# Feed-forward stages: the two halves of an inner chunk's split one tile apart, and other steps for the first gate row

## The reference, cut to what matters

```python
def swiglu(h, w_gate, w_up, w_down):
    return (jax.nn.silu(h @ w_gate) * (h @ w_up)) @ w_down

mod = (jax.nn.silu(c) @ w_ada[l] + b_ada[l]).reshape(B, N_MOD, D)
m = [mod[:, j] for j in range(N_MOD)]
h = modulate(rmsnorm(x, ffn1_pre_g[l]), m[0], m[1])
y = swiglu(h, ffn1_w_gate[l], ffn1_w_up[l], ffn1_w_down[l])
x = x + 0.5 * m[2][:, None, :] * rmsnorm(y, ffn1_post_g[l])
```

## Time and profile before

| | |
|---|---|
| three runs, us | 2525.47, 2531.29, 2531.94 |
| the profiled execution, us | 2531.54 |
| its span, us | 2529.7 |
| granted TensorE clock, mean | 0.991 |
| busy share of the span | PE 96%, PEld 88%, DVE 66%, ACT 48%, POOL 28% |
| DMA over the span | 457.45 MB, 181 GB/s |

### The profile page before, as it was taken

How to read it: one execution, slowest core, us unless ns; L and a number is a source line. 1 busy time by engine, 2 the same in 40 slices (tenths; PEclk the granted TensorE clock), 3 DMA queues, 4 the chain that set the end, 5 groups by cost and what they waited for, 6 DMA issues and landing times.

```text
span 2529.7 us, 40330 instructions
## 1 busy us (share of the span) xinstructions
PE 2439.4 (96%) x16347; PEld 2233.2 (88%) x16347; DVE 1675.0 (66%) x3111; ACT 1204.4 (48%) x1827; POOL 711.8 (28%) x333
## 2 busy tenths in 40 slices
PE   4999899999999999999999999999999999999999
PEld 3997878988889999999888888889999999888887
DVE  6887775546565787899544445664877899644444
ACT  4444665445654444443444445654444444444443
POOL 3111001112025661000344443115663000244443
PEclk9999999999999999999999999999999999999999
DMA  7988444665345554444565665335554444555554
GB/s 282 327 300 308 162 138 151 216 195 171 109 159 170 169 166 154 139 142 142 191 196 192 194 193 194 127 125 186 165 177 157 137 140 142 181 192 193 193 192 165
DMA packets 126589, 457.45 MB, mean 181 GB/s; under 512 B 13974, under 2 KB 16962, under 8 KB 125635
## 3 DMA queue, kind: packets, MB, share of 16 engines
q1 hardware_dynamic: 121442, 441.52, 52.4%
q10 hardware_dynamic: 4048, 8.91, 1.0%
q0 software_dynamic: 912, 4.42, 0.5%
HBM read 451.62 MB, written 5.93 MB: 181 GB/s over the span
## 4 chain that ended last, share of the span: by engine, by line
PE 79%; DVE 6%; ACT 1%; issue 0%; POOL 0%; ACTq 0%; DVEq 0%; POOLq 0%
PE bank L607 24%; PE bank L609 23%; PE bank L608 23%; PE bank L1170 4%; DVE sb L2612 1%; DVE sb L2608 1%; DVE sb L1846 1%; PE bank L955 1%; PE bank L1146 1%; PE bank L816 0%; ACT sb L1213 0%; DVE sb L2615 0%; PE bank L622 0%; PE bank L1098 0%; PE bank L973 0%
## 5 line engine op out<-in xcount | busy, mean ns | idle before, releaser
L607 PE MATMUL bank<-sb,sb 128*128 128x256 f32 (+1 forms) x4744 | 1523.1, 321 | 49.1 <-DVE sb L1846 37.0
L608 PE MATMUL bank<-sb,sb 128*128 128x256 f32 (+1 forms) x4744 | 1497.3, 316 | 0.0
L609 PE MATMUL bank<-sb,sb 128*128 128x256 f32 (+1 forms) x4744 | 1497.2, 316 | 0.0
L1213 ACT ACTIVATE sb<-sb 128x1024 fp32r<-128x1024 f32 x765 | 806.6, 1058 | 1087.1 <-PE bank L609 1079.7
L2720 POOL TENSOR_TENSOR sb<-sb,sb 128x1024 fp32r<-128x1024 f32 x256 | 644.1, 2519 | 1337.6 <-ACT sb L1213 1333.6
L607 PEld LDWEIGHTS bank<-sb,sb 128*128 128x128 f32 x4744 | 911.5, 192 | 118.8 <-issue 35.4
L1846 DVE TENSOR_TENSOR sb<-sb,sb 128x1024 fp32r<-128x1024 f32 x509 | 626.2, 1231 | 559.6 <-ACT sb L1213 558.3
L608 PEld LDWEIGHTS bank<-sb,sb 128*128 128x128 f32 x4744 | 911.9, 192 | 55.2 <-issue 1.0
L609 PEld LDWEIGHTS bank<-sb,sb 128*128 128x128 f32 x4744 | 911.0, 192 | 55.4
L2684 DVE TENSOR_TENSOR sb<-sb,sb 128x1024 fp32r<-128x1024 f32 x64 | 160.0, 2499 | 149.7 <-ACT sb L1802 149.7
L2647 DVE TENSOR_SCALAR sb<-sb,sb 128x128 f32<-128x128 f32 x512 | 142.2, 341 | 0.0
(11 more groups left out here) (274 smaller groups left out, 1238.7 us busy)
## 6 DMA issues: line engine op xcount, KB each, us to landing
sb<-in_peer_down_dram SPq DMA_DIRECT2D x256, 512.0 KB, 3.3
sb<-in_peer_up_dram SPq DMA_DIRECT2D x256, 512.0 KB, 3.3
sb<-in_w_ada_dram SPq DMA_DIRECT2D x72, 512.0 KB, 6.5
sb<-in_hyb_in_dram SPq DMA_DIRECT2D x56, 512.0 KB, 3.4
sb<-in_ffn_gate_dram SPq DMA_DIRECT2D x44, 512.0 KB, 4.3
sb<-in_ffn_up_dram SPq DMA_DIRECT2D x44, 512.0 KB, 5.2
sb<-in_ffn_down_dram SPq DMA_DIRECT2D x44, 512.0 KB, 4.3
sb<-in_mix_in_dram SPq DMA_DIRECT2D x25, 512.0 KB, 4.1
```

Of the source, the lines that this page charges most:

```text
L607: e.matmul(out, a[0], b[0], start=start, stop=False)
L608: e.matmul(out, a[0], b[1], start=False, stop=False)
L609: return e.matmul(out, a[1], b[0], start=False, stop=stop)
L1213: self.e.activation(rr(M.hi[k % NSPLIT]), M.raw[k % NRAW], AF.Copy).then_inc(*self.S.tick("hi", k))
```

## The change

`hidden` is cut in two on both engines that have it. On ScalarE `hidden` keeps silu and a new `hidden_part` has the copy; on VectorE `hidden` keeps the product and `hidden_part` has the remainder. `hidden_part(j - 1)` is called after the second `linear()` of chunk j, so one tile later than before: behind the split of tile 2j+4 and the step of tile 2j+1. After the last chunk both are called in turn. This holds for ffn1 and ffn2. In ffn1 the steps of rows change from (13, 15, 16, 18) to (13, 19, 21, 24). The waits themselves and all instructions stay as they are.

```diff
-    "ffn1": (... ("ada", tuple(range(62))), ("rows", (13, 15, 16, 18))),
+    "ffn1": (... ("ada", tuple(range(62))), ("rows", (13, 19, 21, 24))),
...
 # ScalarE
         self.e.activation(m.sg[j % 3], self.K.bank["hidden", s, j][:, 0:256], AF.Silu).then_inc(*self.S.tick("silu", s, j))
+
+    def hidden_part(self, j):
+
+        m, s = self.m, self.s
         self.wait_ge("hidden", s, j)
         self.e.activation(rr(m.hid_hi[:, j]), m.hd[j % 3], AF.Copy).then_inc(*self.S.tick("hidden_hi", s, j))
...
 # VectorE
-        self.e.tensor_tensor(h, self.K.bank["hidden", s, j][:, 256:512], m.sg[j % 3], ALU.mult).then_inc(
+        self.e.tensor_tensor(m.hd[j % 3], self.K.bank["hidden", s, j][:, 256:512], m.sg[j % 3], ALU.mult).then_inc(
             *self.S.tick("hidden", s, j))
+
+    def hidden_part(self, j):
+
+        m, s = self.m, self.s
         self.wait_ge("hidden_hi", s, j)
-        self.e.tensor_tensor(rr(m.hid_lo[:, j]), h, m.hid_hi[:, j], ALU.subtract).then_inc(*self.S.tick("hidden_lo", s, j))
+        self.e.tensor_tensor(rr(m.hid_lo[:, j]), m.hd[j % 3], m.hid_hi[:, j], ALU.subtract).then_inc(*self.S.tick("hidden_lo", s, j))
...
 # ScalarE and VectorE, ffn
             if j:
                 self.hidden(j - 1)
             self.linear()
+            if j:
+                self.hidden_part(j - 1)
         self.hidden(NFF - 1)
+        self.hidden_part(NFF - 1)
         self.contract(NFF)
```

More of the change, by code:

```diff
@@ L64 @@
 BESIDE = {
-    "ffn1": (("vectors", (0, 1, 2)), ("bias", (0, 6, 7, 8, 14, 15)), ("ada", tuple(range(62))), ("rows", (13, 15, 16, 18))),
+    "ffn1": (("vectors", (0, 1, 2)), ("bias", (0, 6, 7, 8, 14, 15)), ("ada", tuple(range(62))), ("rows", (13, 19, 21, 24))),
     "mix1": (("recurrence", (4, 9, 10, 12, 13, 14, 15, 16, 17, 18, 19, 20, 21, 22, 23)), ("select", tuple(range(9, 21))),
@@ L2080, in hidden @@
         m, s = self.m, self.s
-        h = m.hd[j % 3]
         self.wait_ge("silu", s, j)
```

## The result

| us | before | after |
|---|---|---|
| median | 2530.89 (5 runs, 2525.47 to 2531.94) | 2515.30 (5 runs, 2513.32 to 2516.80) |
| profiled execution | 2531.54 | 2513.32 (the fastest of the five) |
| first feature transpose after the stage (L622) | 255.58 | 240.01 |

The ratio is 0.9941 with the 95% interval 0.9930 to 0.9951: faster by 15.6 us at the medians. The first stage's end moved by 15.57 us. The second feed-forward stage takes what it took (from the feature transposes ahead of it to those behind it, 377.92 to 576.58, 198.66 us; before 393.56 to 592.31, 198.75), so all that the medians show lies in the first.

What follows compares the result with a forecast made beforehand. VectorE was taken to bound the first feed-forward stage's chunks with two modulation tiles, making TensorE wait. Links 6.2, end of inner chunks 3.0 and gate row 3.6 sum to 12.8 us: 2531.5 − 12.8 = 2518.7, say 2519, range 2512 to 2528.

Steps and rivals of the forecast that it cites:

- The bound: First feed-forward stage: VectorE is the bound in chunks with two modulation tiles, 6.42 us against TensorE's 5.76.
- the second rival: First stage: links do not matter, VectorE stays late for another reason (GpSimd's low parts); gate row alone pays, 2527, chance 0.14.
- The sum: First stage: 6.2 + 3.0 + 3.6 = 12.8 us won, of 15.0 that can be won.
- the gate row: First stage, steps moved: TensorE's wait for this row and its slow matmuls go, 4.1 us less 0.5, so 3.6 won.
- The links: First stage's inner chunks: later copy and remainder end both VectorE stalls; eight of nine short waits go, 6.2 us won.
- nine short waits: First stage: TensorE's waits for a VectorE low part, 4.7 us together, 6.8 with the cost behind them.
- the ninth short wait: At 88.90 us, hanging on a weight tile that landed late; of its 0.9 us only 0.3 was taken as won.
- The signs: First stage: no TensorE wait for gate row or GpSimd, few for VectorE; contraction some 13 us earlier; no idle before copy, remainder.
- The end of the inner chunks: GpSimd's low part 47 ready at 11.0, TensorE through tile 46 at 11.3: 4.1 us less 1.1, 3.0 won.
- P: At the end of the inner chunks: the end of tile 42, from which the times there are counted.
- The first rival: First stage: transfers take over; if 320 GB/s is all that holds, 6.6 us won, 2525, chance 0.17.
- The third: First stage, slower: product late behind GpSimd low parts, tiles 17, 23, 29, 35, 41 pay 20.5 us, 2548, chance 0.05.

Runs made afterwards that it cites:

- e3: Changed kernel, but ScalarE's copy stays directly behind silu, so only VectorE's remainder goes one tile later: 2535.17 us, ratio 1.0021 to the kernel before.
- e4: Changed kernel, but VectorE's remainder stays directly behind the product, so only ScalarE's copy goes one tile later: 2517.75 us, ratio 0.9950 to the kernel before.
- e6: Kernel before, with the first stage's low parts of tiles 5 to 53 all on VectorE instead of every sixth on GpSimd: 2520.11 us, ratio 0.9965.
- e2: Changed kernel with the gate row's steps back at (13, 15, 16, 18), so the links alone: 2515.93 us, ratio 0.9947 to the kernel before.
- e1: Kernel before with only the gate row's steps changed to (13, 19, 21, 24), links as before: 2528.19 us, ratio 0.9995 to the kernel before.
- e5: Changed kernel with the gate row's steps (15, 15, 16, 18), computed late so that TensorE must wait: 2520.11 us, ratio 0.9964 to the kernel before.

## Why the prediction was right, and where it was not

**The bound** was read rightly: VectorE in the chunks with two modulation tiles, 6.42 us against 5.76, through the high part that waited behind the copy. e3 and e4 show this cause. It was not the only one: e6 shows that GpSimd's low parts made VectorE late as well, which the sum put at nothing and the second rival named.

**The sum** of 12.8 stands against 15.57 at the stage's end. The 15.0 that could be won were won to the last, and 0.65 more: the first matmuls ran at 1.2 GHz until 49.06 us instead of 50.62 (14 slow ones instead of 21 behind the last wait of the features, 0.093 each). Nothing that TensorE does before that point was changed, and the difference does not belong to the change: the rise scatters from 48.85 to 50.64 us over the ten traces, and e2, with the links of the changed kernel, has 50.64. Why it scatters is not shown. The rest of the distance from 12.8 to 15.0 is the 2.2 us that the working had left over as reserves.

**The step that failed** is the gate row: "4.1 won", with 0.5 left over, 3.6. Alone it is worth 1.7 (e1), and beside the links nothing that can be measured (e2: end 240.24 against 240.01). I priced each wait of TensorE by itself and added them up. They were one debt: VectorE was late, and TensorE paid wherever it next needed something of it. A wait that is taken away while the debt stands comes back as others; with the debt gone the gate row's wait goes too, without its steps being moved. That low part 18 would come 0.2 us before its tile I had worked out for the links apart; with the old links TensorE waits 0.41, 0.89, 0.32 and 1.21 us from 95 to 121 us (e1), the 0.89 for low part 18. So the 3.6 belonged to the links, and the sum came out only because they were short by as much and more: each wait was counted once, whichever edit removed it, and both edits were made together. That is luck.

**The links**, taken at 6.2, are therefore mis-sized: alone they take the stage's end from 255.58 to 240.24, 15.3 us, which is their nine short waits (6.8), the gate row's (4.1), the one at the contraction (4.1) and 0.3. Of the ninth short wait I had kept 0.6; it went as well, though ScalarE still waits 2.88 us for a load at 85.80. A smaller slip: a remainder is not read "44 tiles on". Chunk j's comes after tile 2j+3 and is read at tile 44+j, 41 tiles on for the first chunk and 21 for chunk 20; nothing hung on it.

**The signs.** No wait of TensorE is left, and the stage's contraction begins 11.1 us earlier (185.68 to 174.61) and ends 15.6 us earlier, where 13 was named. "No idle time" before copy and remainder was too much: ScalarE's copy still waits 7 times (10.8 us), VectorE's remainder once (0.5 us). None of it reaches TensorE.

**The end of the inner chunks** went as worked out: with P at 171.73, high part 47 to 8.6 (measured 8.7), GpSimd to 11.0 (11.2), TensorE through with tile 46 at 11.3 (11.3). The margin was kept; that I priced it at 3.0 and not 4.1 was caution. e4 shows how thin it is: there the tile is 1.1 us late.

**The first rival**, transfers, did not come: 342 GB/s over the stage, 385 from 100 to 140 us (at most 1.2 MB of 15.4 the second bias broadcast) with TensorE full. The 320 GB/s at which I let it decide is no limit. The Trainium skill (DMA: Bandwidth & Descriptors, "Where 436 GB/s comes from") has about 358 GB/s from HBM for a core, half of what it gives for a stack. One core runs this kernel, and its 385 for 40 us is above that, so the measurement decides. **The second**, that the links would not matter, is refuted by e2; its observation, that GpSimd's low parts hold VectorE up, is true and was the other source of the debt (e6). **The third** did not come: behind a GpSimd low part the product was in time, and TensorE waits for none.

## What to carry to other kernels

Waits of the bound engine that all lead to one late engine are one debt: find what makes that engine late and price the cure by its balance (work and stalls for each period against the bound engine's period), not wait by wait. An in-order queue that needs a result from the other engine should first issue what is ready, above all what feeds a third engine: moving ScalarE's copy behind the next high part gave 14 of 15.6 us at the stage's end (e4), moving the other side alone lost 5 (e3). And a wait is worth its full price, with the slow clock behind it, only where the waiting engine is the bound.

## What the runs showed of the hardware

TensorE's clock fell to 1.2 GHz after idle times of 2.28 and 2.38 us in the kernel before, 2.60 in e3 and 3.78 in e5: the granted clock is 0.52 from 98.19 to 101.60 us, 0.59 from 202.40 to 206.00 in e3 and 0.50 from 97.79 to 101.00 in e5. After one of 2.27 us in e1 (195.39) the first six matmuls still started 0.23 us apart, and then they came 0.43 apart. After an idle time of 1.70 us (e3, 184.27) the clock stayed; window of e3:

```profile
184.20:187.60 3.40, 3.33 (x28) 3.36 (x29) 2.87 (x5) 0.50 (x2) 0.00 (x0) 1.00 0.62 204
```

So a short wait costs 0.23 us on top and a long one 1.6 to 1.8. Split up, a wait is cheaper only while the pieces are few: the nine short ones of the kernel before cost 2.1 us on top of 4.7, for each us as much as the one of 3.8 in e5 with its 1.6.

GpSimd and VectorE hold each other up in both directions. In the earlier trace rows an 8-column operation of VectorE takes 2.31 us beside GpSimd's low part; in the changed kernel VectorE's operation of that moment started 0.02 us before GpSimd's low part, and GpSimd's took 3.91 us where 2.40 is usual; VectorE's next low part, which started while it ran, took 2.86 instead of 1.22 (timelines of GpSimd and VectorE):

```profile
92.71 3.91 POOL L2735 TENSOR_TENSOR sb<-sb,sb 128x1024 fp32r<-128x1024 f32 x1 [14.15 <-ACT sb L1213]
...
94.84 2.86 DVE L1854 TENSOR_TENSOR sb<-sb,sb 128x1024 fp32r<-128x1024 f32 x1
```
